# A two-layer decoder trunk: conditioning weights read by half rows, low weight halves kept in the slots, opening reordered

## What is computed

```python
    c_act = jax.nn.silu(c)
    for l in range(DEPTH):
        mod = (c_act @ w_ada[l] + b_ada[l])[:, None, :]
        shift1, scale1, gate1, shift2, scale2, gate2 = jnp.split(mod, 6, axis=-1)
        h = x * (1 + scale1) + shift1
        y = hybrid_mixer(h, cos, sin, w_in[l], ...)
        x = layer_norm(DEEPNORM_ALPHA * x + gate1 * y, ln1_g[l], ln1_b[l])
        h = x * (1 + scale2) + shift2
        f = swiglu(h, ...) if l % 2 == 0 else top2_moe(h, ...)
        x = layer_norm(DEEPNORM_ALPHA * x + gate2 * f, ln2_g[l], ln2_b[l])
```

## Time and profile before

| | us |
|---|---|
| median of three runs | 1628.4 |
| lowest and highest | 1620.9, 1629.0 |
| span of the profiled execution | 1621.2 |
| PE, DVE, ACT busy in it | 1513, 1294, 955 |
| opening, up to the first projection | 43.5 |
| first mixer and norm, up to the dense layer | to 195 |
| dense layer | to 420 |
| second mixer, norm, router | to 594 |
| eight experts | to 1600 |

### The profile page before, as it was taken

How to read it: one execution, slowest core, us unless ns; L and a number is a source line. 1 busy time by engine, 2 the same in 40 slices (tenths; PEclk the granted TensorE clock), 3 DMA queues, 4 the chain that set the end, 5 groups by cost and what they waited for, 6 DMA issues and landing times.

```text
span 1621.2 us, 20466 instructions
## 1 busy us (share of the span) xinstructions
PE 1512.8 (93%) x7203; PEld 1242.1 (77%) x7203; DVE 1293.6 (80%) x1529; ACT 955.0 (59%) x1102; POOL 32.4 (2%) x59
## 2 busy tenths in 40 slices
PE   4999699999699779999999999999999999999993
PEld 4686489989486468888888888887887887888883
DVE  6535886666435569999999989999999999999996
ACT  1113233333111248878878878878878878887882
POOL 0000200000200010000000000000000000000000
PEclk9989799999799969999999999999999999999997
DMA  9976178777356329989989998998998998998930
GB/s 324 388 278 205 52 261 292 245 266 271 120 182 232 132 78 371 368 318 368 368 331 359 374 353 325 377 374 305 375 373 308 373 375 307 378 369 314 376 142 30
DMA packets 211564, 471.67 MB, mean 291 GB/s; under 512 B 5544, under 2 KB 30238, under 8 KB 211510
## 3 DMA queue, kind: packets, MB, share of 16 engines
q1 hardware_dynamic: 209316, 466.74, 79.1%
q10 hardware_dynamic: 2194, 4.23, 0.7%
HBM read 469.91 MB, written 1.05 MB: 291 GB/s over the span
## 4 chain that ended last, share of the span: by engine, by line
PE 91%; DVE 6%; issue 1%; ACT 1%; SPq 0%; DMA 0%; DVEq 0%; ACTq 0%
PE ps L1348 23%; PE ps L1350 23%; PE ps L1349 23%; PE ps L1222 5%; PE ps L1425 2%; PE ps L1305 2%; PE ps L1342 2%; PE ps L1212 2%; PE ps L1455 2%; DVE ada_acc L733 1%; PE ps L1180 1%; PE ps L1179 1%; PE ps L1194 1%; DVE yv L790 1%; PE ps L1494 1%
## 5 line engine op out<-in xcount | busy, mean ns | idle before, releaser
L1001 DVE TENSOR_TENSOR w_lo<-raw,w_hi 128x1024 fp32r<-128x1024 f32 x672 | 790.4, 1220 | 45.5 <-ACT w_hi L645 26.6
L645 ACT ACTIVATE w_hi<-raw 128x1024 fp32r<-128x1024 f32 x672 | 705.0, 1063 | 145.9 <-PE ps L1350 144.3
L1348 PE MATMUL ps<-w_hi,h_lo 128*128 128x512 f32 x896 | 357.3, 399 | 3.6 <-DVE h_lo L1095 3.4
L1350 PE MATMUL ps<-w_hi,h_hi 128*128 128x512 f32 x896 | 351.0, 392 | 0.0
L1349 PE MATMUL ps<-w_lo,h_hi 128*128 128x512 f32 x896 | 350.2, 391 | 0.0
L1348 PE MATMUL ps<-w_hi,hid_lo 128*128 128x512 f32 x536 | 209.6, 391 | 0.0
L1350 PE MATMUL ps<-w_hi,hid_hi 128*128 128x512 f32 x536 | 208.7, 389 | 0.0
L1349 PE MATMUL ps<-w_lo,hid_hi 128*128 128x512 f32 x536 | 208.7, 389 | 0.0
L1348 PEld LDWEIGHTS ps<-w_hi,h_lo 128*128 128x128 f32 x896 | 168.9, 189 | 43.8 <-issue 5.4
L1350 PEld LDWEIGHTS ps<-w_hi,h_hi 128*128 128x128 f32 x896 | 168.9, 188 | 36.5
L1349 PEld LDWEIGHTS ps<-w_lo,h_hi 128*128 128x128 f32 x896 | 169.2, 189 | 33.3
(11 more groups left out here) (275 smaller groups left out, 1379.9 us busy)
## 6 DMA issues: line engine op xcount, KB each, us to landing
raw<-in_moe_w_gate_dram SPq DMA_DIRECT2D x56, 2048.0 KB, 7.9
raw<-in_moe_w_up_dram SPq DMA_DIRECT2D x56, 2048.0 KB, 8.8
raw<-in_moe_w_down_dram SPq DMA_DIRECT2D x56, 2048.0 KB, 7.8
raw<-in_w_ada_dram SPq DMA_DIRECT2D x20, 2048.0 KB, 9.1
raw<-in_w_in_dram SPq DMA_DIRECT2D x6, 2048.0 KB, 17.4
raw<-in_ffn_w_gate_dram SPq DMA_DIRECT2D x11, 1024.0 KB, 8.4
raw<-in_ffn_w_up_dram SPq DMA_DIRECT2D x11, 1024.0 KB, 10.9
raw<-in_ffn_w_down_dram SPq DMA_DIRECT2D x11, 1024.0 KB, 9.1
```

The source lines that it names most:

```text
L645: act.activation(w_hi[:, (FF_UNITS + k) % SRING, :], raw[:, moe_slot(m), (k % 4) * UNIT:(k % 4 + 1) * UNIT], ACT.Copy).then_inc(unit_hi, 1)
L1001: dve.tensor_tensor(w_lo[:, q, :], raw[:, moe_slot(m), (k % 4) * UNIT:(k % 4 + 1) * UNIT], w_hi[:, q, :].bitcast(F32), ALU.subtract).then_ ...
L1348: pe.matmul(o, x_lo, hi, start=first, stop=False, skip_group_check=True)
L1350: return pe.matmul(o, x_hi, hi, start=False, stop=last, skip_group_check=True)
```

## The change

Six things change together.

1. A strip is now 512 rows by the 1024 columns of a whole vector (half rows of w_ada, in four chunks), so strips 2v and 2v+1 are the two row halves of vector v. `ada_acc` holds two whole vectors. DVE makes four multiply-adds of 1024 columns per strip.
2. The bias comes in through the accumulator. ACT's new `ada_init(k)` copies 128 rows, 12 of them the biases and the rest zero, scaled by a column of the identity, into the accumulator of vector k, after vector k-2 has been summed and emptied. DVE waits for it (`ada_set`).
3. PE sums once per vector: eight column matmuls for shift or scale, one matmul of 512 columns for each half of a gate, no bias matmul. The places in PE's order change with it.
4. `low[k]` lies on the same memory as slot k (`ring.close()` gives it back to the allocator); DVE writes the low half in place and `w_lo` goes. Slots of these weights are freed by `unit_used`, when PE is done with them. RING stays 7, SRING 4.
5. In the opening c is loaded transposed (1024 single elements) ahead of all, then the weights. The bias, positions, parameter rows and router weights are issued by ACT, the first two behind POOL's clear of the bias rows. x is loaded behind strip 1 instead of 3.
6. PE transposes x before it sums the first vectors.

```diff
+GATES = (2, 5)
+BANK7 = ["params", ("ada", 0, 0, 0), ("ada", 0, 1, 0)]
+BANK7 += [("ada", 0, 2, 0), ("ada", 0, 2, 1), ("ada", 0, 3, 0), ("ssq_conv", 0), ("ada", 0, 4, 0), ("ssq_attn", 0)]
...
+        ring = ExitStack()
+        raw = [sb(f"raw{k}", [P, SLOT], stack=ring) for k in range(RING)]
+        ring.close()
+        low = [sb(f"low{k}", [P, SLOT], F32R) for k in range(RING)]
...
         def strip_src(l, n):
-            return a["w_ada"][l][:, n * 512:(n + 1) * 512].rearrange("(c p) n -> p c n", p=P)
+            vec, kh = n // 2, n % 2
+            return a["w_ada"][l][kh * 512:(kh + 1) * 512, vec * D:(vec + 1) * D].rearrange("(c p) n -> p c n", p=P)
...
-                            (unit_lo, ff_first_unit(s) + 4)))
+                            (unit_used, ff_first_unit(s) + 4)))
...
         def _(sp):
-            sp.dma_start(prm_rows[0:KC, :], a["c"].rearrange("a (k p) -> (a k) p", p=P)).then_inc(prm_loaded, 16)
...
+            sp.dma_start(c_col[:, :], a["c"].rearrange("a (k p) -> p (a k)", p=P),
+                         allow_slow_non_contiguous=True).then_inc(c_loaded, 16)
...
-                if name == ("ada", 0, 3):
+                if name == ("ada", 0, 1):
...
-                        sp.wait_ge(unit_lo, i * E_UNITS + (FF_UNITS + 4 * (m - RING + 1)))
+                        sp.wait_ge(unit_used, i * E_UNITS + (FF_UNITS + 4 * (m - RING + 1)))
...
             pool.memset(ident[:, :], 0.0).then_inc(const_order, 1)
+            pool.memset(ada_bias[:, :], 0.0).then_inc(bias_zero, 1)
...
+            def ada_init(k):
+                if k >= 2:
+                    act.wait_ge(bank7_full, bank7(("ada", (k - 2) // VECS, (k - 2) % VECS,
+                                                   1 if (k - 2) % VECS in GATES else 0)) + 1)
+                act.activation(ada_acc[:, k % 2, :], ada_bias[:, :], ACT.Copy, scale=ident[:, k:k + 1]).then_inc(ada_set, 1)
...
+                k = l * VECS + vec
+                if part == (1 if vec in GATES else 0) and k + 2 < L * VECS:
+                    ada_init(k + 2)
...
+            act.wait_ge(bias_zero, 1)
+            act.dma_start(ada_bias[0:L * VECS, :], a["b_ada"].rearrange("l (v n) -> (l v) n", n=D)).then_inc(bias_loaded, 16)
+            act.dma_start(pos_i[:, :], a["positions"][0].rearrange("(t p) -> p t", p=P),
+                          allow_slow_non_contiguous=True).then_inc(pos_loaded, 16)
+            act.wait_ge(c_loaded, 16)
+            act.activation(c_act[:, :], c_col[:, :], ACT.Silu).then_inc(c_ready, 1)
+            act.wait_ge(ident_ready, 1)
+            act.wait_ge(bias_loaded, 16)
+            ada_init(0)
+            ada_init(1)
+            for name, rows in SMALL:
...
+                act.dma_start(prm_rows[PRM_AT[name]:PRM_AT[name] + L * rows, :], src).then_inc(prm_loaded, 16)
+            act.dma_start(router_w[:, :, :], a["moe_router_w"][0].rearrange("(c p) e -> p c e", p=P)).then_inc(rt_loaded, 16)
...
+            drain_ada(0, 0)
+            drain_ada(0, 1)
             def mixer(l):
...
-                for n in MIX_ADA[l][0] + MIX_ADA[l][1]:
-                    drain_ada(l, n)
+                if l == 0:
+                    drain_ada(0, 2, 0)
+                    drain_ada(0, 2, 1)
+                    drain_ada(0, 3)
+                else:
+                    drain_ada(1, 4)
...
+            def drain_ff_ada(i):
+                l, n = FF_ADA[i][1:]
+                if n % 2:
+                    for part in range(2 if n // 2 in GATES else 1):
+                        drain_ada(l, n // 2, part)
...
             def ada_part(l, n, first, last):
...
+                        if kh == 0:
+                            dve.wait_ge(ada_set, k // 2 + 1)
+                        else:
+                            dve.wait_ge(ada_summed, k)
...
+                    ins = dve.scalar_tensor_tensor(acc, w[:, c, :], c_act[:, 4 * kh + c:4 * kh + c + 1], acc, ALU.mult, ALU.add)
...
-                dve.tensor_tensor(w_lo[:, u % SRING, :], slot_of(name)[:, lo:lo + UNIT],
+                dve.tensor_tensor(low_of(name)[:, lo:lo + UNIT], slot_of(name)[:, lo:lo + UNIT],
                                   w_hi[:, u % SRING, :].bitcast(F32), ALU.subtract).then_inc(unit_lo, 1)
...
-                        ada_part(*FF_ADA[s][1:], 2 * k, 2 * k + 2)
+                        ada_part(*FF_ADA[s][1:], k, k + 1)
...
+            def ada(l, vec, part=0):
+                k = l * VECS + vec
+                pe.wait_ge(ada_summed, 2 * (k + 1))
+                use_bank7(("ada", l, vec, part))
                 acc = ada_acc[:, k % 2, :]
+                if vec in GATES:
+                    m = pe.matmul(ps[:, 7, :], ones[:, :], acc[:, part * 512:(part + 1) * 512], start=True, stop=True)
                 else:
+                    for c in range(KC):
+                        m = pe.matmul(ps[:, 7, c:c + 1], acc[:, c * P:(c + 1) * P], ones[:, 0:1], start=True, stop=True)
...
-            for n in range(4):
-                ada(0, n)
+            turn_input(0)
+            ada(0, 0)
+            ada(0, 1)
...
-                if l == 0:
-                    ada(0, 4)
                 channels(("wc", l), 2).then_inc(zc_mm, 1)
...
-                for n in MIX_ADA[l][0]:
-                    ada(l, n)
+                if l == 0:
+                    ada(0, 2, 0)
                 pe.wait_ge(gb_ready, l + 1)
                 channels(("wu", l), 0).then_inc(zu_mm, 1)
-                for n in MIX_ADA[l][1]:
-                    ada(l, n)
+                if l == 0:
+                    ada(0, 2, 1)
+                    ada(0, 3)
+                else:
+                    ada(1, 4)
...
-                for n in MIX_ADA[l][2]:
-                    ada(l, n)
+                if l == 0:
+                    ada(0, 4)
+                else:
+                    ada(1, 5, 0)
...
+                if l == 1:
+                    ada(1, 5, 1)
...
+            def ff_ada(i, part):
+                l, n = FF_ADA[i][1:]
+                if n % 2 and (part == 0 or n // 2 in GATES):
+                    ada(l, n // 2, part)
...
-                        ada(*FF_ADA[s - 1][1:])
+                        ff_ada(s - 1, 0)
                         pe.wait_ge(silu_done, s)
                     ff_rows(s, 0, 0)
                     if s >= 1:
+                        ff_ada(s - 1, 1)
                         pe.wait_ge(hid_done, s)
                     ff_rows(s, 1, 1)
```

More of the change, by code:

```diff
@@ L287, in load_ada @@
             src, parts = strip_src(l, n), 2 if k < EARLY else 1
-            loads.append((("ada", l, n), [(q * SLOT // parts, (q + 1) * SLOT // parts, KC // parts,
-                                           src[:, q * KC // parts:(q + 1) * KC // parts, :]) for q in range(parts)],
+            loads.append((("ada", l, n), [(q * SLOT // parts, (q + 1) * SLOT // parts, 4 // parts,
+                                           src[:, q * 4 // parts:(q + 1) * 4 // parts, :]) for q in range(parts)],
                           (ada_summed, k + 1)))
@@ L340, in slot_of, with low_of @@
         def slot_of(name):
-            return raw[:, place_of[name], :]
+            return raw[place_of[name]][:, :]
+        def low_of(name):
+            return low[place_of[name]][:, :]
         def wait_load(eng, name):
@@ L465, in link, with drain_ada @@
                 act.wait_ge(act_order, count[0])
-            def drain_ada(l, n):
-                use = bank7(("ada", l, n))
+            def ada_init(k):
[3 more added lines that the diff above has]
+                act.activation(ada_acc[:, k % 2, :], ada_bias[:, :], ACT.Copy, scale=ident[:, k:k + 1]).then_inc(ada_set, 1)
+            def drain_ada(l, vec, part=0):
+                use = bank7(("ada", l, vec, part))
                 act.wait_ge(bank7_full, use + 1)
-                vec, half = n // 2, n % 2
-                if vec in (2, 5):
-                    act.activation((gate1 if vec == 2 else gate2)[:, half * 512:(half + 1) * 512], ps[:, 7, :], ACT.Copy).then_inc(bank7_free, 1)
+                if vec in GATES:
+                    act.activation((gate1 if vec == 2 else gate2)[:, part * 512:(part + 1) * 512], ps[:, 7, :],
+                                   ACT.Copy).then_inc(bank7_free, 1)
                 else:
@@ L475, in drain_ada @@
                     one = vec in (1, 4)
-                    act.activation(modc[:, l, row, 4 * half:4 * half + 4], ps[:, 7, 0:4], ACT.Identity,
+                    act.activation(modc[:, l, row, :], ps[:, 7, 0:KC], ACT.Identity,
                                    bias=ones[:, 0:1] if one else eps[:, 2:3]).then_inc(bank7_free, 1)
+                k = l * VECS + vec
+                if part == (1 if vec in GATES else 0) and k + 2 < L * VECS:
+                    ada_init(k + 2)
             def modulate(v, l, row, last):
@@ L1000, in moe_lo @@
                 dve.wait_ge(unit_hi, i * E_UNITS + (FF_UNITS + k + 1))
[L1001 removed]
+                part = slice((k % 4) * UNIT, (k % 4 + 1) * UNIT)
```

(3 more changed lines are left out.)

161 lines of the change are left out of this document (70 added, 91 removed).

## The result

The changed kernel takes 1587.4 us (median of 4 runs, 1583.7 to 1588.3), the kernel before on the same chip 1626.0 (4 runs): a ratio of 0.977, 95% interval 0.974 to 0.980. The profiled execution has a span of 1585.6 us against 1621.2, so 35.6 us less. The forecast was 1593 and a gain of 35.1. That 35.6 comes so close to 35.1 is luck: the opening gave nothing and the experts became longer, the dense layer and the mixers gave more, and the errors cancel.

The account below looks back on a forecast made before the run. PE, busy 93% of the span, was taken as the bound, with DVE the path in the opening. Gains of 3.6, 10.7, 18.3 and 2.5 sum to 35.1 us, so 1628.4 becomes 1593 us, range 1582 to 1606.

Parts of the forecast that it names:

- 3.6 predicted: Opening: first projection starts at 39.9 instead of 43.53 us; gain 3.6 us, between 1.2 and 5.6.
- I take 4, in the middle: Opening: the positions' load lands 4 us after issue, between 2.2 and 6.6, so DVE starts at 10.7 to 10.9.
- the 13.5 that was named as a sign of being wrong: Opening: the forecast is wrong if DVE's first multiply-add starts after 13.5 us.
- The rule quoted there, a descriptor for each element: Opening: a strided last dim makes 1024 descriptors for c; landing at 9.6 us would still stay inside the bounds.
- 10.7 predicted: First mixer: fewer sums on PE and no clock fall in the third projection; gain 10.7 us, or 8.6 if it falls.
- The wait for ACT's preset: First mixer: DVE's strip 8 waits for vector 4's preset; 3.5 us of cover before PE's value matmuls, so no cost.
- 18.3 predicted: Dense layer: 13.8 us of PE work and 4.5 of half-clock spells saved; gain 18.3 us, between 13.8 and 21.3.
- ACT's parking: Dense layer, two gate steps: ACT waits for PE's second gate half; 1.8 us of cover, else 1 to 3 us lost twice.
- 2.5 predicted: Second mixer: the strips at 493.17 to 498.13 us become one vector; gain 2.5 us.
- nothing predicted: Experts: low halves written into the slots and later load release cost nothing; an expert still takes 126 us.
- Of the rivals, the second: First mixer, gate steps and opening: presets make DVE or PE wait and positions land late; 11 us, 1604; chance 0.13.
- The first, spells that stay as many: PE's clock: half-clock spells stay as many but fall elsewhere, 6.6 us not gained, 1600; chance 0.16.

Follow-up runs that it names:

- pos_first: The changed kernel with the positions' load moved to the front of ACT's queue; 1583.5 us, ratio 0.975.
- order_undone2: The changed kernel with the 16 transposes of x put back behind the second vector's sums; 1587.5 us, ratio 0.979.
- best2: The changed kernel with experts' low halves in their own ring, old SBUF places, early release, positions first, opening's fourth preset behind the modulation; 1574.1 us, ratio 0.971.
- sums_twice: The changed kernel with the column sums of the dense layer's three vectors done twice; 1598.1 us, ratio 0.985.

## Why the prediction was right, and where it was not

**Opening: wrong by its whole size** (3.6 predicted, 0.0 at the second projection). The step that failed is "I take 4, in the middle", with 6.6 us as the upper bound of the positions' landing: it was 8.5, outside the bounds, and DVE's first multiply-add started at 14.86, behind the 13.5 that was named as a sign of being wrong. The row used as the bound was a large load early in the stream, and a small one can take longer. `pos_first` shows that this was the cause: 4.3 us came back with that one load. The rule quoted there, a descriptor for each element, didn't make c late; its 4 KB landed 2.5 us after issue, ahead of all weights. A second fault is that the sum ended at the first projection: until the clock is up, a gain there need not be one behind it (0.7 became 0.0; `order_undone2`: 1.3 became 0.4). The changed opening by itself varies by 0.9 us at the first projection (42.8 to 43.7 in eight profiles). Where the whole chain moved by 3.9 and 4.8 us, in `pos_first` and `best2`, the rise moved with it.

The Trainium skill, DMA: Bandwidth & Descriptors, Queues, rings and completion order, says that each DMA engine takes turns between the queues for which it has work, a packet at a time. The landings of 8.5 us under the stream and 2.5 ahead of it agree in direction; no run here separates turns of packets from other causes.

**First mixer: 10.7 predicted, 15.2 found up to the dense layer.** Right: the strip and the bias matmuls gone, the gate half at 1.0, the third projection at 13.98. Mis-sized: the vector at 2.44, which took 1.78. I had priced eight sums as four sums and four bias matmuls. Eight sums in a row come 0.22 us apart; in the old strip, where sum and bias alternate, each comes 0.31 behind the one ahead. Whether the bias matmul costs more or the alternation does, no run tells. The wait for ACT's preset came as described, with a cover of 1.4 us instead of 3.5, as PE got to the value matmuls in 10.6 us and not in 12.9:

```profile
103.90 5.25 DVE L774 SCALAR_TENSOR_TENSOR ada_acc<-raw,c_act,ada_acc 128x1024 f32<-128x1024 f32 x4 [18.55 <-ACT ada_acc L480]
109.07 1.22 DVE L891 TENSOR_TENSOR cu<-ps,gc_t 128x1024 f32<-128x1024 f32 x1
```

DVE stood 18.6 us and PE's value matmuls at 111.68 waited for nobody. The rest is a spell at half clock behind the strips (116.1 to 119.5 before, gone) and fewer behind the mixer. How many fall there is up to the execution: by the profiles with 127.6 us the stage gains 10.2 and not 15.2.

**Dense layer: 18.3 predicted, 21.0 found**, inside its bounds. The sums left there take 4 x 0.86 + 3 x 1.78 = 8.8 us instead of 4 x 1.03 + 3 x 2.44 = 11.4: 2.6 more. None of the five spells behind strips is left, where I kept two: 3.0 more. And the gate and up products are faster by where the low halves lie: a step without sums takes 16.82 us, where 19.09 less 2.07 for the gate strip leaves 17.02, so 0.2 a step, 2.2 in eleven. Against that, a spell from 198.6 to 202.0 us falls into the second step (1.3 us). And two strips had covered a chain of other engines, so that their removal turns into a wait of PE. At the start of the second step the chain from the end of the first step's products over ACT and DVE to the next low half takes 3.3 us in both kernels (209.61 to 212.88, now 193.94 to 197.20):

```profile
212.88 0.36 PE L1348 MATMUL ps<-h_hi,w_lo 128*128 128x256 f32 x1 [1.07 <-DVE w_lo L942]
```
```profile
197.20 0.35 PE L1393 MATMUL ps<-h_hi,low 128*128 128x256 f32 x1 [2.98 <-DVE low L983]
```

1.9 of that strip's 2.1 us are lost to it. At the layer's end the last strip's removal gave 0.6 of its 2.4 us, because PE then waits for the low half of the hidden tile. In all 18.3 + 2.6 + 3.0 + 2.2 - 1.3 - 1.9 - 1.8 = 21.1.

```profile
377.44 0.50 PE L1393 MATMUL ps<-w_hi,hid_lo 128*128 128x512 f32 x1 [1.51 <-DVE hid_lo L995]
```

The steps are 16.8 and 18.6 us where I gave 17.0 and 19.4, and the gate steps, where I feared ACT's parking, hold no wait of PE's. That PE has no wait at all in this layer was read from steps in its middle and holds neither for its second step nor for its end. The mechanism of the clock, the single columns, is shown by `sums_twice`: eight columns left the clock up in three of three steps, sixteen took it down in three of three. The Trainium skill's rule, TensorE: Matmul & The Clock Gate, Why this matters for your kernels, which names idle gaps, would have left all three at 2.4 GHz, since PE has no gap there; the measurement decides against it as the only cause.

**Second mixer: 2.5 predicted, 5.9 found.** The strips gave 3.3 instead of 2.5, with the true price of a vector; a spell behind them, 498.4 to 501.8 us before, is gone (1.6); and PE has full clock from the start of the first projection (1.8). I had counted neither, and 0.8 went back later.

**Experts: nothing predicted, 6.5 lost.** Each step of the argument held: the subtraction is not slower, the loads are released in time, DVE is not the bound. What failed is one that stands nowhere, that PE's matmuls take the same time wherever their operands lie. The 0.8 us times eight is the largest single loss, and it needed no wait to arise, so no view of waits could have shown it.

Of the rivals, the second was half right (the positions late, the presets harmless). The first, spells that stay as many, is excluded: between the second projection and the experts the clock was at half for 103 us before and for 68 after.

## What to carry to other kernels

When tensors are moved or reused in place, compare PE's matmul spacing before and after, not only the waits: 5.6 ns in 690 cost 6.5 us here, and 7 in 360 gave 2.2. Put small loads that start a chain at the very front of their queue, ahead of the bulk stream on the other queue. Sums that stream single columns should be kept short and apart, and a gain ahead of PE's rise to full clock is to be counted behind it. Before a piece of work is priced as gained, ask whether another engine's chain was hidden under it.

## What the runs showed of the hardware

- Three chained fp32r matmuls of 512 columns mostly take 680 or 687 ns, by where in SBUF the low operand lies, with the same work and clock; of 256 columns 360 or 353, the other way round. An expert had one of two lengths (124.9 or 125.8 us) in all fourteen kernels profiled.
- A load of 1 KB on ACT's queue took 8.5 us to land beside a full weight stream on SP's and behind 48 KB on its own, and 2.5 when issued 0.5 us ahead of both; the 48 KB of bias rows 6.0 to 6.2.
- Behind 1.8 us of single-column matmuls within a busy stretch PE stayed at 2.4 GHz, behind 3.6 us it fell to 1.2 GHz for 3.4 us, in three of three steps, without any idle time.
